# All weight sums of the feed-forward input jobs on VectorE, none on GpSimd

## What is computed

```python
# first block, per layer
u = jnp.square(jax.nn.relu(h @ mlp_w1[i])) @ mlp_w2[i]
h = _layer_norm(DN_ALPHA * h + u, ln2_g[i], ln2_b[i])
...
# second block, twice per layer
h = rms_norm(x, ffn1_pre_g[l])
x = x + FFN_RESID * rms_norm(
    swiglu(h, ffn1_w_gate[l], ffn1_w_up[l], ffn1_w_down[l]), ffn1_post_g[l])

def swiglu(h, w_gate, w_up, w_down):
    return (jax.nn.silu(h @ w_gate) * (h @ w_up)) @ w_down
```

## Time and profile before

| | us |
|---|---|
| median of 3 runs | 2066.53 |
| lowest and highest | 2061.09, 2070.67 |
| the profiled execution, own time | 2056.4 |
| its span in the profile | 2054.6 |
| busy: TensorE / VectorE / GpSimd / ScalarE | 2004.0 / 1088.1 / 636.9 / 345.4 |

### The profile page before, as it was taken

How to read it: one execution, slowest core, us unless ns; L and a number is a source line. 1 busy time by engine, 2 the same in 40 slices (tenths; PEclk the granted TensorE clock), 3 DMA queues, 4 the chain that set the end, 5 groups by cost and what they waited for, 6 DMA issues and landing times.

```text
span 2054.6 us, 31876 instructions
## 1 busy us (share of the span) xinstructions
PE 2004.0 (98%) x12016; PEld 1549.2 (75%) x12016; DVE 1088.1 (53%) x1959; ACT 345.4 (17%) x772; POOL 636.9 (31%) x665
## 2 busy tenths in 40 slices
PE   8999999999999999999999999999999999999998
PEld 6875995468769944699658869994899478869973
DVE  4343866434638655346636544665456636444564
ACT  1332000012420000300024511000200025310000
POOL 0000644310106453134412603434234405312342
PEclk9999999999999999999999989999999999989999
DMA  8422544443144444354435116544744344025453
GB/s 312 142 68 73 191 174 168 147 152 128 56 146 172 164 179 159 120 203 170 164 133 164 53 34 199 174 148 143 268 172 175 145 155 143 11 93 185 166 180 117
DMA packets 82935, 305.46 MB, mean 149 GB/s; under 512 B 9264, under 2 KB 9392, under 8 KB 82416
## 3 DMA queue, kind: packets, MB, share of 16 engines
q1 hardware_dynamic: 80496, 294.93, 40.9%
q0 software_dynamic: 2304, 8.65, 1.2%
HBM read 302.23 MB, written 1.05 MB: 148 GB/s over the span
## 4 chain that ended last, share of the span: by engine, by line
PE 92%; DVE 4%; ACT 1%; DVEq 1%; issue 1%; DMA 0%; POOL 0%; ACTq 0%; SPq 0%
PE psum L439 26%; PE psum L478 21%; PE psum L242 9%; PE psum L867 8%; PE psum L1814 6%; PE psum L2363 4%; PE psum L315 4%; PE psum L302 3%; PE psum L454 3%; PE psum L326 3%; PE psum L1673 1%; PE psum L451 1%; PE psum L283 1%; PE psum L2738 1%; PE psum L1751 0%
## 5 line engine op out<-in xcount | busy, mean ns | idle before, releaser
L439 PE MATMUL psum<-sq,space 128*128 128x128 f32 x2400 | 302.7, 276 | 0.0
L439 PEld LDWEIGHTS psum<-sq,space 128*128 128x128 f32 x2400 | 286.2, 193 | 0.0
L478 PE MATMUL psum<-space,cat 128*128 128x512 f32 x456 | 208.2, 592 | 0.0
L242 PE MATMUL psum<-h,ring 128*128 128x256 f32 x864 | 195.4, 386 | 7.0 <-DMA ring<-in_weights 7.0
L242 PEld LDWEIGHTS psum<-h,ring 128*128 128x128 f32 x864 | 166.7, 194 | 32.6 <-issue 9.7
L478 PEld LDWEIGHTS psum<-space,cat 128*128 128x128 f32 x456 | 86.4, 189 | 109.3 <-issue 109.3
L405 POOL TENSOR_TENSOR space<-ring 128x512 f32<-128x512 f32 x50 | 66.3, 1326 | 316.7 <-PE psum L439 265.4
L478 PE MATMUL psum<-ring,space 128*128 128x512 f32 x304 | 144.2, 594 | 6.8 <-DVE space L424 6.8
L664 POOL TENSOR_TENSOR cat<-space 128x128 f32<-128x128 f32 x76 | 59.6, 784 | 213.3 <-PE psum L478 213.3
L439 PE MATMUL psum<-sq,ring 128*128 128x128 f32 x800 | 107.7, 278 | 9.1 <-DVE space L410 9.1
L478 PEld LDWEIGHTS psum<-ring,space 128*128 128x128 f32 x304 | 56.7, 189 | 78.7 <-issue 66.4
(11 more groups left out here) (411 smaller groups left out, 3302.8 us busy)
## 6 DMA issues: line engine op xcount, KB each, us to landing
ring<-in_weights SPq DMA_DIRECT2D x552, 512.0 KB, 4.1
space<-in_rows POOLq DMA_DIRECT2D x8, 512.0 KB, 8.5
space<-in_gains POOLq DMA_DIRECT2D x6, 512.0 KB, 4.3
const<-in_consts SPq DMA_DIRECT2D x1, 1493.0 KB, 11.0
h<-in_x SPq DMA_DIRECT2D x1, 1024.0 KB, 4.8
x<-in_x_tok SPq DMA_DIRECT2D x1, 1024.0 KB, 15.3
out<-x SPq DMA_DIRECT2D x2, 512.0 KB, 2.6
space<-in_params POOLq DMA_DIRECT2D x2, 509.5 KB, 7.0
```

The source lines that it names most:

```text
L242: last = pe.matmul(out, unit[:, i, :], rhs[:, i, :], start=(i == 0), stop=(i == KD - 1), skip_group_check=True)
L439: last = pe.matmul(out, weights(i), tokens(i), start=(i == 0), stop=(i == 3), skip_group_check=True)
L478: return pe.matmul(k.psum[:, bank, :], lhs, rhs, start=(p == 0), stop=(p == fn.downs - 1), skip_group_check=True)
```

## The change

`in_sums` of odd jobs is called on VectorE, in the order of the jobs, and no longer on GpSimd. Ahead of the first join VectorE makes the sums of jobs 1, 2 and 3 instead of job 2 alone, and after a join those of every job that is due. The semaphore `pool_summed` is gone and `summed` always names `dve_summed`. The four operations themselves, the buffer with its four places and the waits inside `in_sums` stay.

```diff
@@ Ffn.__init__
-        self.dve0 = sum(x[4] // 2 + x[5] for x in before)
-        self.pool0 = sum(x[4] // 2 for x in before)
+        self.dve0 = sum(x[4] + x[5] for x in before)
@@ Ffn.summed
-        if i >= self.jobs:
-            return k.dve_summed, self.dve0 + self.jobs // 2 + i - self.jobs + 1
-        return (k.pool_summed, self.pool0 + i // 2 + 1) if i % 2 else (k.dve_summed, self.dve0 + i // 2 + 1)
+        return k.dve_summed, self.dve0 + i + 1
@@ dve_ffn
-    in_sums(k, b, dve, fn, 2, k.dve_summed)
+    for i in range(1, HELD):
+        in_sums(k, b, dve, fn, i, k.dve_summed)
@@ dve_ffn, after join(q)
         for i in range(ahead - fn.ins, min(ahead, fn.jobs)):
-            if i % 2 == 0:
-                in_sums(k, b, dve, fn, i, k.dve_summed)
+            in_sums(k, b, dve, fn, i, k.dve_summed)
@@ pool_ffn
     pool.wait_ge(k.y_done, 2 * n_in + 2)
-    for i in range(1, fn.jobs, 2):
-        in_sums(k, b, pool, fn, i, k.pool_summed)
     for p in range(fn.downs):
```

More of the change, by code:

```diff
@@ L172, in __init__ @@
         self.dve_summed = self.sem("strassen_sums_by_vector")
-        self.pool_summed = self.sem("strassen_sums_by_pool")
         self.hid_summed = self.sem("strassen_sums_of_hidden")
```

## The result

| | us |
|---|---|
| before, median of 4 runs (lowest, highest) | 2067.99 (2061.09, 2070.67) |
| changed, median of 4 runs (lowest, highest) | 2051.96 (2050.83, 2052.78) |
| ratio, 95% interval | 0.9927 (0.9902 to 0.9953) |
| span of the profiled execution, before and changed | 2054.6, 2048.9 |

The forecast was no change, 2066.5 us, with 2055 as the lower end. It was wrong. One run of the kernel before in the second later series, 2315.5 us at a granted clock of 0.84, is left out of the ratios as a slow one.

The account below looks back on a forecast made before the run. TensorE, busy for 98% of the span, was taken as the bound. Removal 0, starts 0 and steady stage 0, carried to the median of the runs before, gave 2066.5 us, range 2055 to 2078.

Parts of the forecast that it names:

- The value that I take is 0: TensorE's waits for VectorE in three groups: taking sums off GpSimd gains 0, of at most 24.8 us.
- Removed: nothing gained directly: GpSimd's 50 sums, up to 295 us, lie beside TensorE's work; removing them gives nothing directly.
- The 9.1 us on L410 stay: TensorE's two waits for job 0's sums, ungated starts: caused by GpSimd's residual products, so they stay, 4.5 us twice.
- Starts: 0: At all six feed-forward starts, jobs 1 and 3 behind job 0 on VectorE are ready in time: cost 0.
- the residual products stay where they are: GpSimd's residual products at the ungated starts keep their place, before the place from which the sums go.
- The first rival: At six starts GpSimd's hidden sums delay job 1's sums on VectorE by 3.8 us: +22 us, 2089, chance 0.05.
- Steady stage: 0: Later jobs: VectorE's work fits, 5.18 of 6.25 us per ungated job, 9.7 of 12.5 per gated pair; cost 0.
- VectorE 1125 and GpSimd 340 to 370 us: Busy times expected in the profile after: VectorE 1125 us in the middle of 1052 to 1197, GpSimd 340 to 370.
- The level: Zero change was carried to the median of the runs before, 2066.53 us, with runs from 2061.09 to 2070.67.

Follow-up runs that it names:

- residual_late: The changed kernel with GpSimd's residual products in the ungated feed-forwards held until VectorE has made the sums of jobs 0 and 1: 2046.36 us, ratio 0.9920.
- before_again: The kernel before, run again without an edit as a control: 2061.34 us, ratio 0.9991.
- after_again: The changed kernel, run again without an edit as a control: 2055.62 us, ratio 0.9965 to the kernel before.
- after_third: The changed kernel, run once more without an edit for its interval: 2052.05 us, ratio 0.9958 to the kernel before.
- starts_only: The kernel before with only the sums of jobs 1 and 3 of each feed-forward moved to VectorE: 2054.53 us, ratio 0.9964.
- later_only: The changed kernel with the sums of jobs 1 and 3 of each feed-forward kept on GpSimd: 2059.53 us, ratio 0.9995 to the kernel before.
- all_but_one: The changed kernel with job 1's sums in the two ungated feed-forwards kept on GpSimd: 2061.32 us, ratio 0.9996 to the kernel before.
- one_sum: The kernel before with only job 1's sums in the two ungated feed-forwards moved to VectorE: 2058.01 us, ratio 0.9973.
- sums_first: The kernel before with job 1's sums put ahead of the residual products in GpSimd's queue in the ungated feed-forwards: 2047.50 us, ratio 0.9924.

## Why the prediction was wrong

The stretch that decides can be read from every profile: from the request for the rows (the first L2848 or L2842) to the first instruction of job 2 (L451 or L447), in us. Without any wait it is 27.2, as in residual_late.

| profile, ungated start | products begin after | wait for job 0 | wait for job 1 | job 2 begins after |
|---|---|---|---|---|
| before, first | 9.36 | 4.51 | 0 | 34.18 |
| before, second | 8.65 | 4.54 | 0 | 34.82 |
| before_again, first | 10.08 | 2.52 | 0.93 | 32.69 |
| before_again, second | 9.96 | 0.54 | 4.88 | 35.62 |
| changed, first | 10.09 | 2.52 | 0 | 31.59 |
| changed, second | 9.58 | 2.71 | 0 | 31.83 |
| after_again, first | 9.96 | 2.53 | 0 | 31.42 |
| after_again, second | 9.20 | 2.42 | 0 | 29.91 |
| after_third, first | 11.76 | 0 | 1.69 | 29.19 |
| after_third, second | 10.73 | 0 | 1.69 | 29.18 |
| starts_only, first | 9.51 | 4.64 | 0 | 34.28 |
| starts_only, second | 9.24 | 2.36 | 0 | 31.49 |

The mean of the four starts of the kernel before is 34.33, of the six of the changed one 30.52: 3.8 us a start. A part of that is how the rows fell, since two of the four had early rows and none of the six. So I add the profiles of the kernels that differ only in other sums: with job 1's sums on GpSimd behind the products also later_only (32.68, 35.75) and all_but_one (32.69, 35.32), with them on VectorE also starts_only and one_sum (31.66, 29.91). The means of eight and of ten starts are 34.22 and 31.05, 3.2 us a start, 6.3 us for both, near the lower of the 6.1 and 9.7 that the medians of the series show. Of the eight, the two with early rows gained nothing to speak of by the change, as starts_only shows; it is the later ones that gain.

**The step that failed** is "The value that I take is 0, since at each of the places looked at something else was the cause", and behind it the sentence that no wait names a sum on GpSimd. Both were true of the one execution and wrong as an argument. The row that shows it was in the trace of before, and I used GpSimd's start at 225.49 but not its end:

```profile
230.26 1.53 POOL L410 TENSOR_TENSOR space<-ring,space 128x512 f32<-128x512 f32 x1
```

Job 1's sums ended at 231.79 and were read at 234.65, and I took that as slack. But the read stood there only because of the wait ahead of it. Without the 4.51 us wait, job 0 would have been read at 226.13 - 4.51 = 221.62 and job 1 at 227.87: the sums on GpSimd were 3.9 us late and the first wait hid it. With the two in the same stretch, it is by and large the larger of the two delays that counts, and the change takes away most of job 1's. In that execution the larger was job 0's, so there the change alone would have given nothing; where the rows come later, job 1's is the larger, and its price was put at nothing.

**Point by point.** *Removed: nothing gained directly* is wrong for 2 of the 50 sums and, as far as the runs can tell, right for the other 48, as later_only and all_but_one show. *The 9.1 us on L410 stay* was half right: the cause named, the residual products on GpSimd, is the right one (residual_late takes it away and the wait with it), but the size is not a constant; it runs from 0 to 4.54 us in the table's rows of before and changed, and to 4.64 us in starts_only, with the operation of VectorE that the first product meets. *Starts: 0* was right in the profile after, where job 1's sums took 225.83 to 229.62 = 3.79 us against 3.27 forecast and were 2.6 us early, but after_third has 1.69 us: if the rows are late, the residual products meet job 1 on VectorE, which I had ruled out with "the residual products stay where they are". The first rival had the place and the 2.67 us an operation right, but named the hidden sums as the cause, and set its 3.8 us a start against a kernel before without that lateness; in fact the kernel before had it on GpSimd, where it cost up to 4.88 us. *Steady stage: 0* was right: 6.25 us a job, operations of 0.72 to 0.76 us on average where I expected 0.7. *VectorE 1125 and GpSimd 340 to 370 us* came out as 1136.0 and 376.0.

**The level** failed too. The forecast rests on a median of three runs, 2066.53. With 29 to 31 runs the median of before is 2061.7, 4.8 us lower; the spread that I took for the whole, 2061 to 2071, was its upper half. 2061.7 less 6.3 gives 2055.4; the changed kernel measured 2052.0, 2055.6 and 2052.1. Of the 16.0 us between the medians of the first measurement, 6 to 10 came back in the later series; the rest was the luck of four runs each. The profiled execution of before, 10 us below the median, was the hint that the three runs lay high. The range would have held the time with either error alone.

## What to carry to other kernels

A wait of the bound engine hides the lateness of whatever it needs next. So the slack of a moved step is to be measured against the time at which it would be read without the wait ahead of it, and an engine's queue against its last item, not only the one that the wait names. Where a start depends on when a transfer lands, one profile shows one case of it; two executions of the unchanged kernel cost little and would have shown both here. And the order of a queue can be worth more than the engine: putting one job's sums ahead of four products on GpSimd, which also pushed the products back, gained 14 us, moving fifty jobs' sums off it 6 to 10.

## What the runs showed of the hardware

Behind a drain GpSimd stood still until the transfers that it had asked for itself had landed. In sums_first there is a drain between its second and third operation, and 8.31 us of idle time; the third began at 220.52, the last of the four row transfers landed at about 220.0. At the second start a fifth transfer follows the rows (parameters, L2851). There GpSimd stood for 8.89 us until 616.29, and the fifth landed at about 615.96. Between two residual products stands a drain as well. In one_sum the second product of the second start began 3.38 us after the first had ended, and the fifth transfer had landed at about 625.7:

```profile
626.04 2.35 POOL L2870 TENSOR_TENSOR x<-x,space 128x1024 f32<-128x1024 f32 x1 [3.38 <-issue]
```

At the second start of all ten profiles without an added wait, the first operation behind such a drain began 0.3 to 0.4 us after the fifth transfer had landed, at 12.7 to 15.3 us from the request for the rows. No run leaves out the drain or the transfer, so this is a pattern, not a test. A rival is that VectorE's two-input operations kept GpSimd out: in sums_first eight of them in a row ended at 220.73. Against it, the third operation began before that end, and in the first profile of before the second product of the second start began at 619.12, between two operations of such a row (L405 at 618.62, L406 at 619.22).

VectorE was held up for one GpSimd operation at a time, 2.67 to 2.84 us instead of 0.69 beside products of 2.6 us; that is the rule which the prediction weighed (the Trainium skill, "SBUF — State Buffer", section "SBUF: two separate sides"), and the rows agree with it.

A wait can cost TensorE more than its length. After the 4.51 us wait at 226.13 the first block took 2.08 us instead of 1.06, and job 1 was read 8.52 us after job 0 instead of 6.25. Before the wait the granted clock was 1.00, the upper level of 2.4 GHz; from 226.13 to 230 us it was 0.50, the lower level of 1.2 GHz, and from 231 us on 1.00 again. In residual_late, which doesn't wait, it was 1.00 throughout that stretch. The length of the wait alone doesn't settle the price: in after_again the clock was 0.50 for 2 us after the wait of 2.53 us at 226.98 and 1.00 after the one of 2.42 us at 626.94, and job 2 began 4.2 us later than without a wait in the one case and 2.7 us in the other.

The moment at which the feed-forward starts varies as well: the rows were asked for at 204.5 to 211.6 us in the profiles of kernels that are identical up to that point. That may be a part of what spreads the runs, in both kernels; it was not taken apart, and its cause is open.
